# Dense gate and up products of a two-block layer: seven half-size block products per column chunk in place of eight

## What is computed

```python
def _swiglu(h, w_gate, w_up, w_down):
    return (jax.nn.silu(h @ w_gate) * (h @ w_up)) @ w_down
...
        h = _rmsnorm(x, ffn_norm[l])
        if l % 2 == 0:
            j = l // 2
            x = x + _swiglu(h, dense_w_gate[j], dense_w_up[j], dense_w_down[j])
        else:
            j = l // 2
            x = x + _moe(h, moe_router[j], moe_w_gate[j], moe_w_up[j], moe_w_down[j])
```

## Time and profile before

| | |
|---|---|
| median of 3 runs | 1832.71 us (1831.16 to 1833.58) |
| the profiled execution | 1830.57 us, its span 1828.8 us |
| TensorE busy | 1731.1 us, 95% |
| VectorE busy | 389.5 us, 21% |
| ScalarE busy | 278.2 us, 15% |
| GpSimd busy | 98.5 us, 5% |
| dense stage, TensorE | from 515.8 us to the down products at 672.2 us |

### The profile page before, as it was taken

How to read it: one execution, slowest core, us unless ns; L and a number is a source line. 1 busy time by engine, 2 the same in 40 slices (tenths; PEclk the granted TensorE clock), 3 DMA queues, 4 the chain that set the end, 5 groups by cost and what they waited for, 6 DMA issues and landing times.

```text
span 1828.8 us, 24989 instructions
## 1 busy us (share of the span) xinstructions
PE 1731.1 (95%) x10980; PEld 847.7 (46%) x10980; DVE 389.5 (21%) x789; ACT 278.2 (15%) x552; POOL 98.5 (5%) x151
## 2 busy tenths in 40 slices
PE   8999999999999999999899977999998879999977
PEld 4576654456644454556544322444443334444322
DVE  3633323315410000236341000110100001011012
ACT  1201220224310000233211010110101001011011
POOL 0210000006000000024000000000000000000000
PEclk9999999999999999999999999999999989999989
DMA  9732226635144253432659999999999999999996
GB/s 333 244 128 94 93 65 216 241 140 184 47 152 170 92 184 106 167 138 94 240 216 392 410 390 410 408 384 410 383 409 409 382 409 381 409 400 383 410 395 251
DMA packets 169654, 492.43 MB, mean 269 GB/s; under 512 B 15595, under 2 KB 24188, under 8 KB 169285
## 3 DMA queue, kind: packets, MB, share of 16 engines
q1 hardware_dynamic: 161751, 472.30, 68.5%
q0 software_dynamic: 3632, 12.98, 1.9%
q10 hardware_dynamic: 4158, 5.49, 0.9%
HBM read 482.59 MB, written 13.00 MB: 271 GB/s over the span
## 4 chain that ended last, share of the span: by engine, by line
PE 81%; DMA 12%; SPq 2%; DVE 2%; issue 1%; ACT 1%; POOL 0%; ACTq 0%; DVEq 0%; POOLq 0%
PE bank L1271 33%; PE bank L2862 18%; PE bank L2921 7%; DMA ring<-in_moe_w_up 7%; PE bank L2878 7%; PE bank L2931 3%; DMA ring<-in_moe_w_down 2%; PE bank L537 2%; PE bank L612 1%; PE bank L1283 1%; DMA shift_rows<-ring 1%; SPq L2787 1%; PE bank L2894 1%; DMA ring<-shift_rows 1%; PE bank L1849 1%
## 5 line engine op out<-in xcount | busy, mean ns | idle before, releaser
L1271 PE MATMUL bank<-ring,work 128*128 128x512 f32 (+4 forms) x1632 | 670.6, 569 | 5.4 <-DVE work L2206 2.8
L1271 PEld LDWEIGHTS bank<-ring,work 128*128 128x128 f32 x1632 | 304.3, 191 | 340.5 <-issue 317.6
L2862 PE MATMUL bank<-ring,work 128*64 128x512 f32 x1792 | 410.5, 616 | 41.3 <-DMA ring<-in_moe_w_up 35.5
L2862 PEld LDWEIGHTS bank<-ring,work 128*64 128x64 f32 x1792 | 133.2, 142 | 302.1 <-issue 301.3
L2921 PE MATMUL bank<-ring,work 128*64 128x512 f32 x896 | 200.6, 599 | 9.9 <-DMA ring<-in_moe_w_down 9.9
L2921 PEld LDWEIGHTS bank<-ring,work 128*64 128x64 f32 x896 | 63.7, 137 | 134.0 <-issue 134.0
L2878 PE MATMUL bank<-ring,work 128*32 128x256 f32 x2240 | 125.0, 380 | 0.0
L3041 DVE TENSOR_TENSOR work<-work,bank 64x512 f32<-64x512 f32 x56 | 38.7, 692 | 304.7 <-ACT work L2962 295.2
L2878 PEld LDWEIGHTS bank<-ring,work 128*32 128x32 f32 x2240 | 70.9, 110 | 60.8 <-issue 16.2
L3049 DVE TENSOR_TENSOR work<-work,bank 32x256 f32<-32x256 f32 x70 | 29.3, 419 | 221.5 <-ACT work L2971 220.5
L2962 ACT ACTIVATE work<-bank 64x512 f32<-64x512 f32 x56 | 32.9, 588 | 231.5 <-PE bank L2862 231.5
(11 more groups left out here) (408 smaller groups left out, 1135.3 us busy)
## 6 DMA issues: line engine op xcount, KB each, us to landing
ring<-in_moe_w_gate SPq DMA_DIRECT2D x56, 2048.0 KB, 21.2
ring<-in_moe_w_up SPq DMA_DIRECT2D x56, 2048.0 KB, 18.0
ring<-in_moe_w_down SPq DMA_DIRECT2D x56, 2048.0 KB, 21.4
ring<-in_w_in SPq DMA_DIRECT2D x20, 2048.0 KB, 8.3
ring<-in_w_out SPq DMA_DIRECT2D x6, 2048.0 KB, 7.7
ring<-in_dense_w_gate SPq DMA_DIRECT2D x5, 2048.0 KB, 8.1
ring<-in_dense_w_up SPq DMA_DIRECT2D x5, 2048.0 KB, 7.8
ring<-in_dense_w_down SPq DMA_DIRECT2D x5, 2048.0 KB, 7.7
```

The lines of the kernel that those rows point to most:

```text
L1271: mm = pe.matmul(banks(j)[:, 0:width], x[:, k0 + kt, tt * P:(tt + 1) * P], w[:, kt, c0:c0 + width], start=first and n == 0, stop=last and ...
L2862: mm = pe.matmul(out[rows, :], xgT[:, half * tiles + k, 0:64], w[n][:, k, cols], start=(half == 0 and k == 0), stop=last)
```

## The change

For a chunk of columns, gate and up of both token halves are written as one product of 2x2 block matrices. Left: rows are the late half (tokens 128 to 255) and the early half (0 to 127), columns are features 0 to 511 (`lo`) and 512 to 1023 (`hi`). Right: rows are `lo` and `hi`, columns are the gate and the up weights. Eight block products of four matmuls each become seven (Winograd's form of Strassen's scheme):

- `first` is late-lo by gate-lo, `second` late-hi by gate-hi, both in one bank; `fourth` is early-hi by `t4`; `fifth` and `third` are `s1` by `t1` and `s4` by up-hi, both in one bank; `sixth` is `s2` by `t2`; `seventh` is `s3` by up-hi minus up-lo.
- `s1` to `s4` are sums of blocks of `uT`, formed once by VectorE. `t1`, `t2`, `t4` and the difference of the up halves (written over up-lo in its ring slot) are sums of weights, formed for every chunk by GpSimd, each of 128 x 2048 float32 (128 x 1024 for the last chunk). The `t` tiles have two buffers; buffer c waits for `second` of chunk c-2.
- ScalarE copies the `first` bank out before `second` adds to it; VectorE adds copies and banks together to the four wanted results.

```diff
+def part_product(core, pe, j, left, right, first=True):
+    tiles, width = right.shape[1], right.shape[2]
+    for k in range(tiles):
+        mm = pe.matmul(core.banks(j)[:, 0:width], left[:, k, :], right[:, k, :], start=(first and k == 0),
+                       stop=(k == tiles - 1), skip_group_check=True)
+        if k == 0:
+            core.give_weights_back(mm)
+    return mm
...
-def feed_forward(core, plan, lead, after, hid, hidT):
+def feed_forward(core, plan, lead, after, room, spare, spare_left, hidT):
     nc, h, uT, banks = core.nc, core.h, core.uT, core.banks
     widths = [w for _, w in FF_COLS]
     n_cols, parts = len(widths), plan["down"]
     split = len(parts) - 2
+    quarter = KD // 2
+    hid = [room.take(NT, BANK) for _ in range(2)]
+    s1, s2, s3, s4 = (room.take(quarter, P) for _ in range(4))
+    t1, t2, t4 = ([r.take(quarter, BANK) for r in (spare, room)] for _ in range(3))
+    base, both, plain = (spare.take(BANK) for _ in range(3))
+    early, late = slice(0, P), slice(P, SEQ)
+    lo, hi = slice(0, quarter), slice(quarter, KD)
+    a11, a12, a21, a22 = uT[:, lo, late], uT[:, hi, late], uT[:, lo, early], uT[:, hi, early]
+    weights_summed, rows_summed, first_done, first_copied, fifth_done, fifth_added, gate_raised, hid_ready = (
+        core.new_semaphore(n) for n in ("weights_summed", "rows_summed", "first_done", "first_copied", "fifth_done",
+                                        "fifth_added", "gate_raised", "hid_ready"))
...
+        def weights(c):
+            gate, up = core.view(plan["gate"][c]), core.view(plan["up"][c])
+            return gate[:, lo, :], gate[:, hi, :], up[:, lo, :], up[:, hi, :]
+        def first(c):
+            core.wait_weights(pe, plan["gate"][c])
+            banks.enter(pe, J["first", c])
+            part_product(core, pe, J["first", c], a11, weights(c)[0]).then_inc(first_done, 1)
+        def second(c):
+            pe.wait_ge(first_copied, c + 1)
+            banks.fill(part_product(core, pe, J["first", c], a12, weights(c)[1], first=False))
+            core.spent(plan["gate"][c])
+        def third(c):
+            core.wait_weights(pe, plan["up"][c])
+            pe.wait_ge(rows_summed, 4)
+            pe.wait_ge(fifth_added, c + 1)
+            banks.fill(part_product(core, pe, J["fifth", c], s4, weights(c)[3], first=False))
+            core.spent(plan["up"][c])
+        def fourth(c):
+            pe.wait_ge(weights_summed, 4 * c + 4)
+            banks.enter(pe, J["fourth", c])
+            banks.fill(part_product(core, pe, J["fourth", c], a22, t4[c % 2][:, :, 0:widths[c]]))
+        def fifth(c):
+            pe.wait_ge(weights_summed, 4 * c + 1)
+            pe.wait_ge(rows_summed, 1)
+            banks.enter(pe, J["fifth", c])
+            part_product(core, pe, J["fifth", c], s1, t1[c % 2][:, :, 0:widths[c]]).then_inc(fifth_done, 1)
+        def sixth(c):
+            pe.wait_ge(weights_summed, 4 * c + 2)
+            pe.wait_ge(rows_summed, 2)
+            banks.enter(pe, J["sixth", c])
+            banks.fill(part_product(core, pe, J["sixth", c], s2, t2[c % 2][:, :, 0:widths[c]]))
+        def seventh(c):
+            pe.wait_ge(weights_summed, 4 * c + 3)
+            pe.wait_ge(rows_summed, 3)
+            banks.enter(pe, J["seventh", c])
+            banks.fill(part_product(core, pe, J["seventh", c], s3, weights(c)[2]))
         def turn_hid(c):
             for tt in range(NT):
-                pe.wait_ge(*banks.left(J["up", c, tt]))
+                pe.wait_ge(hid_ready, 2 * c + tt + 1)
...
         lead.turned(pe, 0)
-        product("gate", 0, 0)
+        fourth(0)
         lead.turn(pe, 1)
-        product("up", 0, 0)
+        fifth(0)
         lead.turned(pe, 1)
-        product("gate", 0, 1)
-        product("up", 0, 1)
+        first(0)
+        sixth(0)
+        seventh(0)
+        second(0)
+        third(0)
         for c in range(1, n_cols):
-            for name in ("gate", "up"):
-                for tt in range(NT):
-                    product(name, c, tt)
+            first(c)
+            sixth(c)
+            seventh(c)
+            fifth(c)
+            fourth(c)
+            second(c)
+            third(c)
             turn_hid(c - 1)
...
+        def copy_first(c):
+            act.wait_ge(first_done, c + 1)
+            if c:
+                act.wait_ge(hid_ready, 2 * c)
+            nc.scalar.copy(base[:, 0:widths[c]], banks(J["first", c])[:, 0:widths[c]]).then_inc(first_copied, 1)
+        def gate_early(c):
+            rows = hid[c % 2][:, 0, 0:widths[c]]
+            act.wait_ge(*banks.left(J["fourth", c]))
+            lead.scaled(act, 0)
+            nc.scalar.activation(rows, rows, ACT.Silu, scale=lead.scale[:, 0:1]).then_inc(gate_raised, 1)
+        def gate_late(c):
+            j = J["first", c]
             act.wait_ge(*banks.ready(j))
-            lead.scaled(act, tt)
-            banks.leave(nc.scalar.activation(hid[c % 2][:, tt, 0:widths[c]], banks(j)[:, 0:widths[c]], ACT.Silu,
-                                             scale=lead.scale[:, tt:tt + 1]), j)
+            lead.scaled(act, 1)
+            banks.leave(nc.scalar.activation(hid[c % 2][:, 1, 0:widths[c]], banks(j)[:, 0:widths[c]], ACT.Silu,
+                                             scale=lead.scale[:, 1:2]), j)
...
+    @core.block.gpsimd
+    def _(pool):
+        pool.wait_ge(*spare_left)
+        for c in range(n_cols):
+            gate, up = core.view(plan["gate"][c]), core.view(plan["up"][c])
+            one, two, four = (t[c % 2][:, :, 0:widths[c]] for t in (t1, t2, t4))
+            core.wait_weights(pool, plan["gate"][c])
+            core.wait_weights(pool, plan["up"][c])
+            if c >= 2:
+                pool.wait_ge(*banks.ready(J["first", c - 2]))
+            pool.tensor_tensor(one, up[:, lo, :], gate[:, lo, :], ALU.subtract).then_inc(weights_summed, 1)
+            pool.wait_ge(weights_summed, 4 * c + 1)
+            pool.tensor_tensor(two, up[:, hi, :], one, ALU.subtract).then_inc(weights_summed, 1)
+            pool.wait_ge(weights_summed, 4 * c + 2)
+            pool.tensor_tensor(up[:, lo, :], up[:, hi, :], up[:, lo, :], ALU.subtract).then_inc(weights_summed, 1)
+            pool.wait_ge(weights_summed, 4 * c + 3)
+            pool.tensor_tensor(four, gate[:, hi, :], two, ALU.subtract).then_inc(weights_summed, 1)
+            pool.wait_ge(weights_summed, 4 * c + 4)
...
-        def times_up(c, tt):
-            j, rows = J["up", c, tt], hid[c % 2][:, tt, 0:widths[c]]
+        def with_base(c):
+            w, rows = widths[c], hid[c % 2][:, 0, 0:widths[c]]
+            j = J["sixth", c]
+            dve.wait_ge(first_copied, c + 1)
             dve.wait_ge(*banks.ready(j))
-            dve.wait_ge(*banks.left(J["gate", c, tt]))
-            banks.leave(dve.scalar_tensor_tensor(out=rows, in0=banks(j)[:, 0:widths[c]], scalar=lead.scale[:, tt:tt + 1],
-                                                 in1=rows, op0=ALU.mult, op1=ALU.mult), j)
+            banks.leave(dve.tensor_tensor(base[:, 0:w], base[:, 0:w], banks(j)[:, 0:w], ALU.add), j)
+            dve.wait_ge(*banks.left(j))
+            j = J["seventh", c]
+            dve.wait_ge(*banks.ready(j))
+            banks.leave(dve.tensor_tensor(both[:, 0:w], base[:, 0:w], banks(j)[:, 0:w], ALU.add), j)
+            dve.wait_ge(*banks.left(j))
+            dve.wait_ge(fifth_done, c + 1)
+            dve.tensor_tensor(plain[:, 0:w], both[:, 0:w], banks(J["fifth", c])[:, 0:w], ALU.add).then_inc(fifth_added, 1)
+            j = J["fourth", c]
+            dve.wait_ge(*banks.ready(j))
+            banks.leave(dve.tensor_tensor(rows, both[:, 0:w], banks(j)[:, 0:w], ALU.add), j)
+            dve.wait_ge(fifth_added, c + 1)
+            dve.wait_ge(gate_raised, c + 1)
+            dve.scalar_tensor_tensor(out=rows, in0=plain[:, 0:w], scalar=lead.scale[:, 0:1], in1=rows, op0=ALU.mult,
+                                     op1=ALU.mult).then_inc(hid_ready, 1)
+        def times_late(c):
+            w, rows = widths[c], hid[c % 2][:, 1, 0:widths[c]]
+            j = J["fifth", c]
+            dve.wait_ge(*banks.ready(j))
+            banks.leave(dve.tensor_tensor(base[:, 0:w], base[:, 0:w], banks(j)[:, 0:w], ALU.add), j)
+            dve.wait_ge(*banks.left(j))
+            dve.wait_ge(*banks.left(J["first", c]))
+            dve.scalar_tensor_tensor(out=rows, in0=base[:, 0:w], scalar=lead.scale[:, 1:2], in1=rows, op0=ALU.mult,
+                                     op1=ALU.mult).then_inc(hid_ready, 1)
...
+        for c in range(2):
+            dve.wait_ge(*banks.left(lead.uses[0][c]))
+        dve.tensor_tensor(s1, a21, a22, ALU.add).then_inc(rows_summed, 1)
         lead.gained(dve, 1)
-        times_up(0, 0)
-        times_up(0, 1)
-        for c in range(1, n_cols):
-            for tt in range(NT):
-                times_up(c, tt)
-            turned(c - 1)
+        dve.wait_ge(rows_summed, 1)
+        for c in range(2):
```

(34 more changed lines are left out.)

27 lines of the change are left out of this document (15 added, 12 removed).

## The result

The changed kernel takes 1817.85 us against 1832.61 us. This median of four holds one slow execution, of 2557 us at a TensorE clock of 0.65; the median of the other three is 1817.44 (1817.13 to 1818.25). The ratio without it is 0.9919, 95% interval 0.9902 to 0.9935, which is a gain of 11.9 to 18.0 us. It is faster, as forecast, but by 14.8 us (15.2 by the three) where the sum said 18.9, and both medians lie just above the range, which ended at 1817.3. The profiled execution took 1817.13 us, its span 1815.3.

The account below looks back on a forecast made before the run. TensorE was taken to bound the dense stage; removed products give 18.9 us, waits and giving weights back were priced 0, so 1832.7 - 18.9 = 1813.8 us, range 1811.8 to 1817.3.

Parts of the forecast that it names:

- The removed product: Dense stage on TensorE: each chunk loses one product of eight, 5 x 3.43 + 1.73 = 18.9 us less.
- GpSimd's dates: Dense stage: weight sums of 4.2 us each, 16.8 per chunk, end 16 to 17 us before the tightest demand in chunks 1 to 4.
- the price 0 of contention: Mixer's end and chunk 0: VectorE's work beside GpSimd's sums makes TensorE wait nowhere; 0 us.
- the second rival: Mixer's end and chunk 0: GpSimd's and VectorE's two-input sums exclude each other on ports; 1815 to 1817 us, chance 0.13.
- T = 5.1: One GpSimd sum of 2048 elements at 5.1 us, the bound from a row where one input is repeated.
- T = 4.2: One GpSimd sum of 2048 elements at 4.2 us, the value taken for the forecast; no stall under exclusion.
- The recorded 2.5 us for T = 5.1: Chunk 0: under exclusion with sums of 5.1 us, `plain` ends at 539.8, wanted at 537.3, so TensorE stalls 2.5 us; time 1816.3.
- The rows show pairs that overlap in part: Argument against full exclusion of VectorE's and GpSimd's two-input sums, from rows of sums of 256 columns.
- giving weights back late: Dense stage: up weights of chunk c+2 issued up to some 3 us later in a chunk's course; price 0.

Follow-up runs that it names:

- r2: The changed kernel with GpSimd's sums for chunk 0 waiting until the mixer's two value scalings on VectorE are done; 1816.12 us.
- r4: The changed kernel with chunk 0's GpSimd sums waiting for the mixer's value scalings and chunk 1's for `s1` to `s4`; 1816.29 us.
- r8: The changed kernel with each GpSimd sum as two instructions of 1024 elements; 1814.20 us.
- r10: The changed kernel with GpSimd's sums in halves and those of chunk 0 also behind the mixer's value scalings; 1815.89 us.
- r7: The changed kernel with a second instruction of the same size ahead of every GpSimd sum; 1864.34 us.
- r3: The changed kernel with GpSimd's sums for chunk 1 waiting until VectorE has formed `s1` to `s4`; 1817.44 us.

## Why the prediction came out as it did

**The removed product** was right at 18.9 us. r2, r4, r8 and r10, which have no new idle time, shorten the stretch by 18.85.

**GpSimd's dates** were right in kind. A sum takes 4.51 us alone and 4.83 beside a blocked VectorE instruction, and I took 4.2, from a row of 1024 elements doubled. The Trainium skill's GPSIMD Engine Reference, section "3.1 Elementwise — side-by-side cycle accounting", has 4.497, and the trace agrees with it and not with my choice. No product waited for the sums themselves, and r7 confirms that at some factor up to two above this they become the bound.

**The step that failed** is the price 0 of contention between GpSimd's sums and VectorE's two-input instructions. It measured 2.35 us of TensorE's time, in two places that the second rival worked through. First, in the mixer: "L2352 of 490.03 and of 491.57, held by sums and with one more held instruction between them, would end by 492.1 and 503.7 at T = 5.1, wanted by the transposes at 496.91 and 504.21: no stall". The second scaling did end at 503.0, 501.5 on the old clock (the times of the kernel before, 1.55 us less than here in the mixer, 3.0 less in the dense stage). But I asked only who wants the scaled rows and not what stands behind the held instruction on VectorE: the copy of the first turned tile, which TensorE wants after the first 8 of the 16 records that follow the transposes of 496.91, at 500.8 on the old clock. In the kernel before it had 2.5 us to spare:

```profile
497.54 0.69 DVE L2195 COPY work<-bank 128x512 f32<-128x512 f32 x1 [5.28 <-PE bank L1283]
```

It cost 1.45 us. Second, in chunk 0: `s3` "531.2" at T = 5.1, against a demand of 530.4, and 529.4 at T = 4.2. With sums of 4.5 to 4.8 us it came at 533.99, 531.0 on the old clock; 0.5 us of wait, 0.9 with what followed. The recorded 2.5 us for T = 5.1 has a slip: three sums, each with a held instruction behind it, end at 519.6 + 3 x 5.79 = 537.0 and not at 537.7, which makes it 1.8. And the sums began at 524.01, 521.0 on the old clock, not at 519.6, since the weights took 9.0 us to land and not 7.8. I had taken one landing time from one profile as fixed; r2, held just as long, lost nothing here with a landing of 7.6.

**The evidence I set against it** was misread. "The rows show pairs that overlap in part": I took this as a weaker kind of contention. A part of each short instruction does overlap in the new rows too: a held one of 0.69 us adds only 0.33 to the next sum. That this is all there is to the 256-column pairs is argued and not shown. In a wait of 4.7 us such a part counts for little, and r8 shows that the length of the sum ahead is what counts. So the chance of 0.13 for this rival was too low, and its price, taken only from chunk 0, left out the mixer's part, although the mixer's was the larger.

**The other steps** came as written: `fifth` had `s1` in time (522.2, start 523.1), `third` waited at most 0.2 us, giving weights back late cost nothing, the clock stayed at 1.00, and DMA had room until the experts.

**The rest of the miss** stays open. With 2.35 us for contention the forecast would have been 1816.15, inside the range; the measured 1817.4 to 1817.85 lies 1.3 to 1.7 us above that, and no run locates it. Spread between executions is enough to hold it: three pairs of medians of these same two kernels gave 15.2, 16.8 and 15.2 us, and 16.55 lies inside the interval of 11.9 to 18.0 us, while 18.9 doesn't. My range had 1.5 us of spread under the forecast; it needed as much above the second rival.

## What to carry to other kernels

When work goes to an idle engine, ask for each instruction that the other engine runs beside it whether the two share a port, and if they do, charge the full length of the newcomer to the other engine's whole queue, not only to the result of the held instruction. The cure is cheap: shorter instructions on the engine with time to spare (r8, both places), or a start behind the critical one's two-input work (r2 for the mixer's 1.45 us, r3 for chunk 0's 0.9). A wait that comes and goes with the landing of a load, as chunk 0's does, is not cured by an edit in whose profile it happens to be away: check the landing before crediting the edit. Seven products for eight did pay their arithmetic price exactly, 18.85 of 18.9 us in the stretch once no new wait was left, since TensorE was the only bound and GpSimd's 18 to 19.5 us of sums fitted into a chunk's 24.9.

## What the runs showed of the hardware

A VectorE instruction of 512 columns with both inputs in SBUF waits for the whole of a GpSimd sum that began before it: 4.67 to 5.00 us for 0.69 behind sums of 4.8 us, 2.5 to 2.8 behind sums of 2.35, and the held one adds 0.33 us to the next sum (4.84 for 4.51). With one input in a bank it takes 0.68 us beside a sum. After some waits of 2 to 7 us of TensorE the granted clock was between 0.57 and 0.68 for the next eight records, and after others 1.00 (r7). One and the same load of 2 MB, at the same place of the program, landed in 7.6 to 7.9 us in seven profiles and in 9.0 to 9.4 in six.
